# A new memory map for a two-layer transformer kernel: weight parts low in the partition, the tiles they are multiplied with high

## What is computed

```python
proj = hn @ w_in[l]                       # w_qi, w_ki, w_qb, w_kb, w_vb, w_qa, w_ka, w_va, w_g
merged = jax.nn.sigmoid(ga) * (ya @ w_proj_a[l]) + jax.nn.sigmoid(gb) * (yb @ w_proj_b[l])
x = x + gate1[:, None, :] * (merged @ w_out[l])          # w_o
# PEER: scores of 128 x 128 keys, top 16 of each head, then
pre = jnp.einsum('cd,chkd->chk', hc, u[ec])
coef = gc * jax.nn.gelu(pre, approximate=False)
f = jnp.einsum('chk,chkd->cd', coef, v[ec])
# second layer: hybrid_mixer, memory_cross_attention, conv_ffn, each on rmsnorm(x)
```

## Time and profile before

| | |
|---|---|
| runs, median (lowest to highest) | 1455.45 us (1455.34 to 1460.9) |
| the profiled execution | 1460.37 us, its span 1458.5 us |
| matmuls recorded | 10406 |
| TensorE busy, weight loads busy | 1412.5 us, 1313.7 us |
| VectorE, ScalarE, GpSimd busy | 1095.6, 837.0, 358.9 us |
| read from HBM | 262.88 MB, 183 GB/s over the span |

### The profile page before, as it was taken

The page is one execution under the profiler, slowest core; times in us unless marked ns, Lnnn a source line. Parts: engine busy times, 40 slices in busy tenths (PEclk is TensorE's granted clock), DMA queues, the critical chain, the costliest instruction groups (busy, mean ns, idle before and its releaser), DMA issues.

```text
span 1458.5 us, 25878 instructions
## 1 busy us (share of the span) xinstructions
PE 1412.5 (97%) x10406; PEld 1313.7 (90%) x10406; DVE 1095.6 (75%) x1903; ACT 837.0 (57%) x1447; POOL 358.9 (25%) x227
## 2 busy tenths in 40 slices
PE   7999999899999999999999999999999999899997
PEld 5998898899999999999988888887888899799997
DVE  7788887567889888899756666677668667787762
ACT  4555774444454677777545454465456666776641
POOL 3216201233445100000122322244322221432200
PEclk9999999999999999999999999999999999999998
DMA  9768775446654544444556666665666535375630
GB/s 381 270 196 281 245 232 174 156 148 183 184 182 149 175 147 144 150 146 143 154 171 220 196 193 193 217 194 177 193 205 252 175 114 177 96 237 182 193 103 30
DMA packets 73721, 268.24 MB, mean 184 GB/s; under 512 B 8401, under 2 KB 9730, under 8 KB 72834
## 3 DMA queue, kind: packets, MB, share of 16 engines
q1 hardware_dynamic: 71280, 256.41, 55.5%
q10 hardware_dynamic: 1426, 7.56, 1.4%
q0 software_dynamic: 896, 2.62, 0.5%
HBM read 262.88 MB, written 3.67 MB: 183 GB/s over the span
## 4 chain that ended last, share of the span: by engine, by line
PE 81%; DVE 11%; ACT 4%; DMA 1%; issue 1%; POOL 1%; DVEq 0%; ACTq 0%; POOLq 0%
PE bank L604 81%; DVE split L1818 3%; DVE ada_acc L1853 2%; ACT split L1288 1%; DMA ringb<-in_w_ada 1%; DVE PR L2265 0%; POOL H L2637 0%; DVE rT L1904 0%; DVE PR L2268 0%; PE bank L777 0%; POOL split L2610 0%; DMA far<-in_w_g 0%; DVE H L2359 0%; DMA vecs<-in_vecs 0%; DVE PA L2069 0%
## 5 line engine op out<-in xcount | busy, mean ns | idle before, releaser
L604 PE MATMUL bank<-H,split 128*128 128x256 f32 x5928 | 744.3, 286 | 14.9 <-DVE mod L1834 5.4
L604 PEld LDWEIGHTS bank<-H,split 128*128 128x128 f32 x5928 | 722.1, 193 | 22.1 <-issue 9.4
L1288 ACT CAST split<-ringb 128x1024 fp32r<-128x1024 f32 x350 | 365.6, 1046 | 288.1 <-PE bank L604 276.4
L604 PE MATMUL bank<-split,H 128*128 128x512 f32 (+1 forms) x1728 | 392.0, 389 | 3.3 <-DVE H L2359 1.8
L2610 POOL TENSOR_TENSOR split<-ringb,split 128x1024 fp32r<-128x1024 f32 x91 | 226.5, 2489 | 675.2 <-ACT split L1288 675.2
L1818 DVE TENSOR_TENSOR split<-ringb,split 128x1024 fp32r<-128x1024 f32 x259 | 328.4, 1271 | 84.1 <-ACT split L1288 84.0
L604 PEld LDWEIGHTS bank<-split,H 128*128 128x128 f32 x1728 | 322.4, 189 | 71.1 <-POOL split L2610 2.5
L2359 DVE TENSOR_TENSOR H<-PR,H 128x256 fp32r<-128x256 f32 x128 | 137.1, 1073 | 107.0 <-ACT H L1627 107.0
L1818 DVE TENSOR_TENSOR split<-far,split 128x1024 fp32r<-128x1024 f32 x77 | 100.0, 1308 | 33.8 <-ACT split L1288 33.7
L1288 ACT CAST split<-far 128x1024 fp32r<-128x1024 f32 x89 | 93.0, 1047 | 54.6 <-PE bank L604 44.4
L1603 ACT ACTIVATE PR<-bank 128x512 f32<-128x512 f32 (+31 forms) x59 | 28.7, 486 | 78.8 <-PE bank L604 78.8
(11 more groups left out here) (298 smaller groups left out, 1258.6 us busy)
## 6 DMA issues: line engine op xcount, KB each, us to landing
ringb<-in_u SPq DMA_DIRECT2D x128, 512.0 KB, 3.7
ringb<-in_v SPq DMA_DIRECT2D x128, 512.0 KB, 4.4
ringb<-in_w_ada SPq DMA_DIRECT2D x28, 512.0 KB, 5.4
far<-in_w_up SPq DMA_DIRECT2D x26, 512.0 KB, 4.2
far<-in_w_ada SPq DMA_DIRECT2D x20, 512.0 KB, 5.7
ringb<-in_w_up SPq DMA_DIRECT2D x17, 512.0 KB, 4.8
ringb<-in_w_pq SPq DMA_DIRECT2D x16, 512.0 KB, 4.2
far<-in_w_dn SPq DMA_DIRECT2D x14, 512.0 KB, 3.9
```

The source lines that it names most:

```text
L604: return TE.matmul(o, l, r, start=start, stop=stop, skip_group_check=True)
L1288: S.copy(buf(m)[0], slots[P.slot[m]]).then_inc(hi_done, 1)
```

## The change

Only addresses move, and one wait. A second stack (`upper`) takes bytes from the top of the partition down. The buffers of the weight parts come first in the lower stack, the tiles that are multiplied with them go to the upper one or to the end of the lower. `split4` has three pairs for four (the ring never used the last), two unused gaps push act_t up, and PB falls into PM and PX. Bytes of a partition, before and after:

| tile | before | after |
|---|---|---|
| split | 32896 to 57472 | 16512 to 41088 |
| split1 | 212928 to 221120 | 41088 to 49280 |
| split5 | 219328 to 227520 | 41088 to 49280 |
| split4 | 161984 to 194752 | 49280 to 73856 |
| H | 65664 to 82048 | 212992 to 229376 |
| Yb, Ya | 187328 to 203712 | 144256 to 160640 |
| Ym | 116928 to 133312 | 131200 to 147584 |
| MH | 133312 to 149696 | 114816 to 131200 |
| act_t | 116928 to 161984 | 102528 to 147584 |
| ringb | 16512 to 32896 | 188416 to 204800 |
| xT | 57472 to 65664 | 204800 to 212992 |
| PR (rows of the u and v stage, 1024 bytes each) | 92352 to 223424 | 41088 to 172160 |

Since far2 now lies over rows 109 and up of PR, which the v stage reads until its coefficients are made, SP's wait before a load into far2 rises from coefficient 73 to one between 114 and 128, by slot. The diff:

```diff
+        def upper(name, shape, dt=F32):
+            return ctx.enter_context(nc.sbuf_tensor(name, shape, dt, side="right"))
...
-        ringb = sb("ringb", [128, 4, UNIT])
         split = sb("split", [128, 3, 2, UNIT], F32R)
-        xT = sb("xT", [128, 8, T])
-        H = sb("H", [128, 2, 8, T], F32R)
+        H = upper("H", [128, 2, 8, T], F32R)
+        xT = upper("xT", [128, 8, T])
+        ringb = upper("ringb", [128, 4, UNIT])
...
         with ExitStack() as ph:
+            split1 = sb("split1", [128, 1, 2, UNIT], F32R, where=ph)
             far = sb("far", [128, 3, UNIT], where=ph)
             PA = sb("PA", [128, 20672], where=ph)
             Yb = sb("Yb", [128, 2, 4, T], F32R, where=ph)
             Ya = sb("Ya", [128, 2, 4, T], F32R, where=ph)
             zbuf = sb("zbuf", [128, 2, 3, 384], where=ph)
-            split1 = sb("split1", [128, 1, 2, UNIT], F32R, where=ph)
...
-        far2 = sb("far2", [128, 6, UNIT])
+        split5 = sb("split5", [128, 2, UNIT], F32R)
+        far2 = upper("far2", [128, 6, UNIT])
+        sc_g = upper("sc_g", [128, 1024])
         with ExitStack() as ph:
+            PM = sb("PM", [128, 12288], where=ph)
+            PX = sb("PX", [128, 4096], where=ph)
+            MH = sb("MH", [128, 2, 8, T], F32R, where=ph)
             Ym = sb("Ym", [128, 2, 8, T], F32R, where=ph)
-            MH = sb("MH", [128, 2, 8, T], F32R, where=ph)
-            PB = sb("PB", [128, 16384], where=ph)
-            sc_g = sb("sc_g", [128, 1024], where=ph)
-            split5 = sb("split5", [128, 2, UNIT], F32R, where=ph)
         with ExitStack() as ph:
+            split4 = sb("split4", [128, 3, 2, UNIT], F32R, where=ph)
+            sb("gap0", [128, 1024], where=ph)
+            ftmp = sb("ftmp", [128, 4, 768], where=ph)
+            sb("gap1", [128, 3072], where=ph)
             act_t = sb("act_t", [128, 2, 22, T], F32R, where=ph)
-            split4 = sb("split4", [128, 4, 2, UNIT], F32R, where=ph)
-            ftmp = sb("ftmp", [128, 4, 768], where=ph)
...
                 if where == "far2":
-                    y.wait_ge(c_lo, 73)
+
+                    y.wait_ge(c_lo, min(128, 114 + 4 * (P.slot[n] - 7)) if P.slot[n] >= 7 else 73)
```

More of the change, by code:

```diff
@@ L373, in sem @@
             return ctx.enter_context(nc.semaphore(name))
-        ringb = sb("ringb", [128, 4, UNIT])
+        def upper(name, shape, dt=F32):
+            return ctx.enter_context(nc.sbuf_tensor(name, shape, dt, side="right"))
         split = sb("split", [128, 3, 2, UNIT], F32R)
-        xT = sb("xT", [128, 8, T])
-        H = sb("H", [128, 2, 8, T], F32R)
[L380 to L385, removed]
+        H = upper("H", [128, 2, 8, T], F32R)
+        xT = upper("xT", [128, 8, T])
+        ringb = upper("ringb", [128, 4, UNIT])
+        cst = upper("cst", [128, 768])
+        vecs = upper("vecs", [128, A["vecs"].shape[1]])
+        mod = upper("mod", [128, 48])
+        sm = upper("sm", [128, 160])
+        cond = upper("cond", [128, 8])
+        rT = upper("rT", [128, 5, T])
         banks = [ctx.enter_context(nc.psum_tensor(f"bank{i}", [128, 512], F32)) for i in range(8)]
         with ExitStack() as ph:
+            split1 = sb("split1", [128, 1, 2, UNIT], F32R, where=ph)
             far = sb("far", [128, 3, UNIT], where=ph)
@@ L466, in build @@
         cf = [(Hf[:, i * 512:i * 512 + 256], Hf[:, i * 512 + 256:i * 512 + 512]) for i in range(8)]
-        xkT, xv, bmm, mqT, mkT, mv, ccT, uT, ctmp, gqk, goT, gv, lrT, sc_b, gt = pieces(
-            PB, 512, 512, 3072, 1024, 1024, 1024, 512, 516, 512, 512, 512, 512, 256, 3072, 2560)
+        xkT, xv, bmm = pieces(PX, 512, 512, 3072)
+        mqT, mkT, mv, ccT, uT, ctmp, gqk, goT, gv, lrT, sc_b, gt = pieces(
+            PM, 1024, 1024, 1024, 512, 516, 512, 512, 512, 512, 256, 3072, 2560)
         mem3, bmm3 = tri3(bmm[:, 0:2048], 8), tri3(bmm, 8)
@@ L479, in build @@
         bufs1 = bufs + [(split1[:, 0, 0, :], split1[:, 0, 1, :])] + 3 * [None] + last_buf
-        bufs2 = bufs + [(split4[:, i, 0, :], split4[:, i, 1, :]) for i in range(4)] + last_buf
+        bufs2 = bufs + [(split4[:, i, 0, :], split4[:, i, 1, :]) for i in range(3)] + [None] + last_buf
         XL0 = P.at["w2_xl", 0]
```

## The result

Slower by about one per cent: 1472.7 us, the median of five runs (1470.87 to 1476.91), against 1458.12 for the kernel before in the same session (1455.34 to 1460.9); ratio 1.0105 with an interval of 1.008 to 1.013. The profiled execution of the changed kernel took 1472.7 us too (span 1471.0). That of before was one of its longer ones (1460.37), so that by the profiles 12.4 us are to be explained from the span's start to the last matmul, and 14.6 by the medians.

A forecast was written before the change was run, and what follows sets the result against it. TensorE was taken as the bound, through the pitch of successive matmuls. Terms of -10.0 and +2.8 us, all others 0, sum to -7.2, giving 1448 us from the median 1455.45; range 1418 to 1457.

The forecast's parts named there:

- The bound: Whole kernel: TensorE, busy 97% of the span, with 81% of the chain on the matmul line, then L604.
- No change for VectorE, ScalarE and GpSimd: These three engines keep their instructions; the subtraction's shortest times are equal from low and high buffers: 0 us.
- SP's wait: Second block's weight loads: SP holds far2 loads for coefficient 114 to 128, for 73 before; cost 0.
- the second term: 631 matmul intervals in w_pa, w_pb, w_dn and parts of the second block go from 113.3 to 117.8 ns: +2.8 us.
- Act_t is all at one value: Sign to look for: act_t's matmuls all at one value, with no alternation.
- The step that failed: Reading of the trace: duration 283 marks operands on one side of the partition, 276 and 279 to 281 a crossed pair.
- Rival 3: Delays come from something that only went along with the side; pitches stay, 1455.4 us; chance 0.07.
- 4511 matmuls from 120.0 to 117.8: First term, intervals of 256-column matmuls across stages: 4511 fall from 120.0 to 117.8 ns, -10.0 us.
- The v stage: 1536 matmuls of 512 columns, H now high: expected 0 at 226.7 ns, range 0 to 5.7 us.
- Rival 2: V stage at 229 takes 3.6 us back: 1451.9, chance 0.15; at 236 throughout, 1462.5 or 1470, chance 0.12.
- point of no return: Rival 2's v-stage pitch at which the change turns to a loss: 231.4 ns.
- The side step: Weights low, moving high: 113.3 ns after a both-high unit, 117.8 after a gap; so 117.8 was taken for the change.

The follow-up runs named there:

- the second repaired map: The changed kernel's map with streaming tiles at difference 192 from their weight parts and v's coefficients at 0, against the kernel before: 1437.34 us, ratio 0.987.

## Why the prediction was wrong

**What it got right.** The bound (L611 is on 83% of the chain), and that pitch is what counts: the whole loss lies in L611's groups. The pitch does depend on addresses: matmul pitch and the durations of matmul and weight load change together with the distance of the two starts, 283 and 192 at difference 0, 275 and 188 at 112. The page "SBUF — State Buffer" of the Trainium skill, section "Who interferes with whom", says that TensorE never waits on anyone; yet the six kernels in the changed map differ in start addresses alone, and their times go from 1431 to 1473 us. No change for VectorE, ScalarE and GpSimd, and none from SP's wait: both held, the latter by the kernel with H high at difference 0. The pitches of 113.3 in w_pa, w_pb and w_dn were lost, as the second term had it, but to 120.0, not 117.8: their difference is now 0. Act_t is all at one value, as said, the wrong one.

**The step that failed** is the sentence "So 283 marks a pair on one side, 276 and 279 to 281 a crossed pair." Each row behind it is right; what was read off them is not. The trace of before has two classes of pairs, and two properties that split them alike: side, and start address modulo 256. The addresses that show the second were in the prediction's own lines: 32896 and 65664 are both 128 modulo 256, 195520 and 212928 both 192. So its cost for the new pairs, 117.8 in place of 120.0, had no ground: what was measured for them is 120.0 in u and 234.3 in v, at differences 96 and 160 that the kernel before never had. Rival 3 named this case, "something that only went along with the side", but gave it 0.07 and took its time to be that of before, as if pitches would stay; yet an unknown property moves with the addresses too, in either direction. The table's 32 bytes hid the rest: at the printed 212992, H would have been at 0, a difference of 128, and the 96 bytes of the real map could not have been read from it. The best that the rows allowed was to say that the new pairs' price was not to be read from this trace.

**By terms.** 4511 matmuls from 120.0 to 117.8, -10.0 us: measured 0, they stayed at 120.0, as a mean of pitches from 115 to 125. The 631 from 113.3, +2.8: w_up and w_dn alone lost 2.2 and the second block 1.6, in part from 117 to 118. The v stage, 0 with a range to 5.7: measured 7.5 ns each, 234.3 less 226.8, which times 1536 is 11.5 us; over the last 1512 the stage is 10.6 us longer (0.7 less by fewer long pitches), and its start at full clock gave 1.4 back, which leaves the 9.2. The prediction's range for it rested on w_vb's unit from split1, which "settled" at 229; that is difference 64, which has 229 in every kernel. The value taken, 0, was argued from a row of 256 columns, and the two widths rank differences differently: 192 is among the fast ones for 256 (115 to 118) and among the slow ones for 512 (233.3). Rival 2 had place and sign right, but it too laid the price on the side: with H as high and the residue restored, v is at 226.8. Its point of no return, 231.4, was passed, and that the time came out near its "1470 if the others gain nothing" is luck in so far as the reason is another.

**The side step that held, and what is open.** The prediction read from the trace that a crossed pair behind a unit with both parts high is at 113.3, and at 117.8 behind a gap. In residues this is difference 64 behind difference 0, and over the 17 kernels that have this difference the starts bear it out: 132 of 141 such stretches are under 115; behind 128, none of 122; behind a gap, 54 of 504. For 192 it is the other way, and less sure: 1 of 162 behind 0, 23 of 26 behind 128, some 260 of 400 behind a gap. For the changed kernel it was idle, having neither difference. What settles it behind a gap is open: with difference 192 all through, u's first part is at 113.4 in one kernel and at 117.5 in two others, its last part at 116.8 in the first and at 114.9 and 113.8 in the others. That one kernel's executions differ in this (the second repaired map ran from 1436.03 to 1445.3) is argued from the spread, not shown. Open too is why these differences and not others: no run looks inside the memory.

## What to carry to other kernels

When two tiles feed one TensorE stream, lay out their start addresses modulo 256 on purpose, for each product by itself: here 112 between streaming and loaded operand for 256 float32r columns and 0 for 512, 1.7% under the kernel before without touching an instruction of TensorE, and a pad of a few words sets it. Before a map is redrawn for side or distance, tabulate the residues of every operand pair before and after; if a property in the trace has only two classes, list everything else that splits them the same way. And take the addresses from the allocated program, not from sums of sizes: 32 bytes were enough here.

## What the runs showed of the hardware

Mean pitch in ns of consecutive float32r matmuls, by start of the streaming operand less start of the loaded one, modulo 256, over all kernels here. Only stretches of one kind at full clock were counted; "x" is the largest count within one kernel, and a value with a small count is from one or two units.

| difference | 256 columns | 512 columns |
|---|---|---|
| 0 | 119.9 (x6046) | 226.7 to 226.8 (x1617); 228.2 to 228.5 where the loaded operand's residue changes |
| 16 | 118.0 (x4099) | 227.6 (x14) |
| 32 | 116.8 (x4139) | 233.1 (x14) |
| 48 | 118.3 (x4129) | 232.0 (x14) |
| 64 | 116.3 to 117.8 (x5093); 114 to 115.8 where most stretches stand behind one at 0 | 228.9 (x118) |
| 80 | 118.3 (x496) | not seen |
| 96 | 119.9 to 120.0 (x5152) | 233.3 (x6) |
| 112 | 113.4 to 113.9 (x6178) | not seen |
| 128 | 118.6 to 118.9 (x4130) | 232.4 (x1511) |
| 144 | 119.8 (x58) | 233.3 (x118) |
| 160 | 117.4 to 118.1 (x516) | 234.3 (x1628) |
| 176 | 118.7 (x21) | 232 to 233 (x10) |
| 192 | 114.9 to 117.8 (x6159) | 233.3 (x1626) |
| 208 | 118.9 (x237) | 233.3 (x75) |
| 224 | 118.3 (x220) | 233.3 (x1581) |
| 240 | 117.2 (x237) | 233.3 (x75) |

At 112 a stretch of over 100 matmuls is at 113.4 to 113.7, and one of 23 at up to 115.8; at 64 and 192 nearly all are at 113.3 or 117.8, which makes the means between. No stretch of 20 or more was under 113.3, or under 226.7, twice that. Durations follow (283 and 192 for matmul and load at difference 0, 276 at the low value, 275 and 188 at 112), so a tile view shows most classes at once. The mean pitch alone does not: 120.0 came at difference 0 from a duration of 283 every time, and at 96 from durations spread between 278 and 286. The same 128 x 256 tile kept its pitch wherever on the partition it lay (from 65664 and from 212864), as long as the difference held.
